# Mamba-2 scan in a fused diffusion block: masks joined to the decay matmuls, loads released by their last readers, skip term added by VectorE

## The reference, cut to what matters

```python
y = xs * lp["ssd_d"]                                   # the skip term
for d in range(2):                                     # forward, and backward on flipped tokens
    lower = jnp.tril(...)
    decay_in = jnp.exp(jnp.where(lower, a_cum[..., :, None] - a_cum[..., None, :], -jnp.inf))
    cb = jnp.einsum("bclgn,bcsgn->bgcls", cc, bc)
    y_diag = jnp.einsum("bgcls,bgecls,bcsgep->bclgep", cb, decay_in, xc)
    y_off = jnp.einsum("bclgn,cbgepn,bgecl->bclgep", cc, h_in, jnp.exp(a_cum))
    y = y + y_diag + y_off
```

## Time and profile before

| | |
|---|---|
| Median of 3 runs | 2537.04 us (2533.92 to 2537.75) |
| Profiled execution | 2539.05 us, span 2537.3 us |
| TensorE busy | 2397.6 us, 94% |
| VectorE busy | 1629.5 us, 64% |
| ScalarE busy | 940.6 us, 37% |
| GpSimd busy | 268.9 us, 11% |
| First instruction of the scan proper | 805.7 us |
| Last VectorE operation of the scan | 904.25 us |

### The profile page before, as it was taken

How to read it: one execution, slowest core, us unless ns; L and a number is a source line. 1 busy time by engine, 2 the same in 40 slices (tenths; PEclk the granted TensorE clock), 3 DMA queues, 4 the chain that set the end, 5 groups by cost and what they waited for, 6 DMA issues and landing times. The chain is left out here.

```text
span 2537.3 us, 30702 instructions
## 1 busy us (share of the span) xinstructions
PE 2397.6 (94%) x12041; PEld 1937.5 (76%) x12041; DVE 1629.5 (64%) x1679; ACT 940.6 (37%) x1099; POOL 268.9 (11%) x260
## 2 busy tenths in 40 slices
PE   6999899899999999999999999999599999999994
PEld 2468777678888978788787788868588888888882
DVE  7453389733344755324975536668888888888876
ACT  5133310233323533001112000031277777777764
POOL 0000000000143300000000001100012112121210
PEclk8999999999999999999999999999699999999997
DMA  5431155312344323111111115533699999999965
GB/s 203 164 124 42 47 190 179 111 46 84 116 150 138 100 65 104 44 52 50 42 50 38 42 50 168 180 140 117 258 360 368 368 357 366 360 371 390 385 265 204
DMA packets 93583, 437.12 MB, mean 172 GB/s; under 512 B 17080, under 2 KB 28616, under 8 KB 78762
## 3 DMA queue, kind: packets, MB, share of 16 engines
q1 hardware_dynamic: 64714, 349.02, 37.5%
q0 software_dynamic: 28768, 86.69, 9.9%
HBM read 401.12 MB, written 55.51 MB: 180 GB/s over the span
## 5 line engine op out<-in xcount | busy, mean ns | idle before, releaser
L390 PE MATMUL ps<-uT_upper_rest,ring_rest 128*128 128x512 f32 x1280 | 504.7, 394 | 0.0
L390 PE MATMUL ps<-uT_upper_rest,mix_upper 128*128 128x512 f32 x768 | 307.4, 400 | 9.9 <-DVE mix_val L2401 5.3
L390 PE MATMUL ps<-uT_rest,mix_upper 128*128 128x512 f32 x768 | 306.4, 399 | 0.0
L390 PEld LDWEIGHTS ps<-uT_upper_rest,ring_rest 128*128 128x128 f32 x1280 | 240.6, 188 | 61.1
L390 PEld LDWEIGHTS ps<-uT_upper_rest,mix_upper 128*128 128x128 f32 x768 | 145.5, 189 | 47.5 <-DVE mix_val L2401 5.7
L390 PEld LDWEIGHTS ps<-uT_rest,mix_upper 128*128 128x128 f32 x768 | 145.3, 189 | 33.0 <-issue 0.5
L1833 ACT ACTIVATE mix_gates<-ps 128x1024 f32<-128x1024 f32 x24 | 24.7, 1027 | 384.3 <-PE ps L390 367.3
L1884 DVE TENSOR_TENSOR mix_prod<-mix_gates,ps 128x1024 f32<-128x1024 f32 x24 | 29.3, 1221 | 211.1 <-PE ps L390 211.1
L2932 PE MATMUL ps<-ex_u_raw_rest,uT_rest 128*128 128x256 f32 x560 | 157.0, 280 | 0.0
L2930 PE MATMUL ps<-ring_rest,uT_rest 128*128 128x256 f32 (+1 forms) x416 | 135.1, 325 | 3.1 <-DVE uT_rest L3295 2.4
L2930 PE MATMUL ps<-ex_upper,uT_rest 128*128 128x256 f32 (+1 forms) x424 | 135.4, 319 | 0.0
(11 more groups left out here) (477 smaller groups left out, 5549.1 us busy)
## 6 DMA issues: line engine op xcount, KB each, us to landing
sb_spare<-in_ex_g SPq DMA_DIRECT2D x35, 2048.0 KB, 10.0
ex_u_raw<-in_ex_u SPq DMA_DIRECT2D x35, 2048.0 KB, 10.6
sb_merged<-in_ex_d SPq DMA_DIRECT2D x35, 2048.0 KB, 9.4
ring<-in_conv SPq DMA_DIRECT2D x32, 512.0 KB, 3.4
ring<-in_w_gate SPq DMA_DIRECT2D x32, 512.0 KB, 3.4
mix_piece<-in_w_late POOLq DMA_DIRECT2D x32, 512.0 KB, 5.2
ring<-in_w_ssd SPq DMA_DIRECT2D x20, 512.0 KB, 3.3
ring<-in_w_mod SPq DMA_DIRECT2D x16, 512.0 KB, 4.3
```

What stands on the lines that cost most here:

```text
L390: last = self.nc.tensor.matmul(out, weight, x[:, k, lo:hi], start=(k == 0 and n == 0), stop=(k == kt - 1 and n == 2))
```

## The change

Four things are changed.

1. *Masks.* Partitions 64 to 127 of `rows` now hold a constant, minus BIG on the diagonal of each 64-column block, and the weights `allowed(d, f)` hold ones for the row part and a 0/1 pattern for the mask part. One matmul gives mask and decay together, for one direction, four heads and half of the tokens (4 runs of 64 columns); a segment is one direction and four heads, two matmuls. The number of segments, banks and exponentials stays; their order becomes forward and backward alternately by four heads. The rows are loaded in three pieces. The second mask sum still waits for the last exponentials, the first for four segments instead of three. One segment (u = 3) moves ahead of `diagonal(n - 1, 1)`.
2. *Loads.* SP waits for each tile's last reader: `b_chan` and `c_chan` for `off_mm`, `b_tok` for `state_mm`, `xs` for `diag_mm` and `skip_ready`.
3. *Skip.* `skipped` goes; VectorE adds `skip` to `off` in SBUF, an eleventh operation per chunk, between backward off and the sum into y.
4. *Preparation.* `eye`, `ones` and `never` go; VectorE fills `rows` in two operations and `allowed` in seven.

The diff, cut to its core:

```diff
-        eye, ones = at_byte("eye", late + 36864, [P, P], F32R), at_byte("ones", late + 37376, [P, P], F32R)
-        never = at_byte("never", late + 37888, [P, 2, PAIR], F32R)
+
+        allowed_at = at_byte("allowed", late + 36864, [P, 2, 2, P], F32R)
+
+        def allowed(d, f):
+            return allowed_at[:, d, f, :]
...
-                    else:
-                        sp.wait_ge(y_done, n - 1)
-                    load_state(sp, n % 2, chunk(n), in_state[n % 2])
+                        load_state(sp, 1, chunk(1), in_state[1])
+                        load_out(sp, 1, in_out[1])
+                        continue
+                    sp.wait_ge(off_mm, 2 * (n - 1))
                     load_out(sp, n, in_out[n % 2])
+                    sp.wait_ge(state_mm, FIRST + n - 1)
+                    load_tok(sp, n % 2, chunk(n), in_state[n % 2])
+                    sp.wait_ge(diag_mm, 2 * (n - 1))
+                    sp.wait_ge(skip_ready, n - 1)
+                    load_xs(sp, n % 2, chunk(n), in_state[n % 2])
...
-                    pe.wait_ge(in_rows[u // 3], 16 * (n + 1))
-                    for d in range(2):
-                        out = ps[:, at_bank, d * PAIR:(d + 1) * PAIR]
-                        nc.tensor.matmul(out, eye[:, :], never[:, d, :], start=True, stop=False)
-                        mm = nc.tensor.matmul(out, ones[:, :], rows[:, d, u * PAIR:(u + 1) * PAIR], start=False, stop=True)
+                    quad, d = u // 2, u % 2
+                    pe.wait_ge(in_rows[quad], 16 * (n + 1))
+                    out = ps[:, at_bank, :].rearrange("p (h f t) -> p h f t", h=4, f=2)
+                    given = rows[:, d, quad * QUAD:(quad + 1) * QUAD].rearrange("p (h f t) -> p h f t", h=4, f=2)
+                    for f in range(2):
+                        mm = nc.tensor.matmul(out[:, :, f, :], allowed(d, f), given[:, :, f, :], start=True, stop=True)
                     mm.then_inc(seg_mm, 1)
...
-                def skipped(n, q):
-                    pe.wait_ge(skip_ready, n + 1)
-                    nc.tensor.matmul(ps[:, 3 + q, 0:half], k.const("ident"), skip[:, q * half:(q + 1) * half],
-                                     start=True, stop=False)
-
                 def diagonal(n, q):
                     pe.wait_ge(mixed, 2 * n + q + 1)
                     pe.wait_ge(in_state[n % 2] if n else state_first, 32 * max((n + 1) // 2, 1))
                     for e in range(6):
                         h = 6 * q + e
                         mm = nc.tensor.matmul(ps[:, 3 + q, e * HD:(e + 1) * HD], grow_f[:, n % 2, h, :],
-                                              xs[:, n % 2, h * HD:(h + 1) * HD], start=False, stop=(e == 5))
+                                              xs[:, n % 2, h * HD:(h + 1) * HD], start=True, stop=True)
...
-                pe.wait_ge(rounded, 4)
+                pe.wait_ge(rounded, 8)
                 segments(0, 0)
                 segments(0, 1)
                 pe.wait_ge(turned_ready, reads_until(items - 1) + 2)
                 segments(0, 2)
                 forward_out(0)
+                segments(0, 3)
...
-                    segments(n, 3)
                     segments(n, 4)
                     pe.wait_ge(off_read, 2 * n + 1)
                     states_out(n, 1)
                     segments(n, 5)
                     if n:
                         pe.wait_ge(y_done, n)
-                    skipped(n, 0)
                     diagonal(n, 0)
...
-                    skipped(n, 1)
+                    if n + 1 < CHUNKS:
+                        segments(n + 1, 3)
                     diagonal(n, 1)
...
-                    if m == convs + 2:
-                        act.wait_ge(raw_turned, 1)
-                        nc.scalar.copy(eye[:, :], k.const("ident")).then_inc(rounded, 1)
-                        nc.scalar.copy(ones[:, :], k.ones[:, :]).then_inc(rounded, 1)
...
                 def grow(n, u):
+                    quad, d = u // 2, u % 2
                     act.wait_ge(seg_mm, 6 * n + u + 1)
-                    if n == 0 and u == 4:
+                    if n == 0 and u == 5:
                         act.wait_ge(last_out, 32)
-                    if n >= 2:
-                        act.wait_ge(diag_mm, 2 * (n - 2) + u // 3 + 1)
-                    if n >= 1:
-                        act.wait_ge(summed, 2 * (n - 1) + u // 3 + 1)
-                    for d in range(2):
-                        for e in range(2):
-                            h = 2 * u + e
-                            dst = grow_b[:, h, :] if d else grow_f[:, n % 2, h, :]
-                            at_col = d * PAIR + e * P
-                            ins = nc.scalar.activation(dst, ps[:, SEG[(6 * n + u) % 3], at_col:at_col + P], ACT.Exp,
-                                                       bias=at("bias", chunk(n), d, h, h + 1))
+                    if n >= 2 and d == 0:
+                        act.wait_ge(diag_mm, 2 * (n - 2) + min(quad, 1) + 1)
+                    if n >= 1 and d == 1:
+                        act.wait_ge(summed, 2 * (n - 1) + min(quad, 1) + 1)
+                    for e in range(4):
+                        h = 4 * quad + e
+                        dst = grow_b[:, h, :] if d else grow_f[:, n % 2, h, :]
+                        ins = nc.scalar.activation(dst, ps[:, SEG[(6 * n + u) % 3], e * P:(e + 1) * P], ACT.Exp,
+                                                   bias=at("bias", chunk(n), d, h, h + 1))
                     ins.then_inc(grown, 1)
...
-                    nc.vector.tensor_scalar(rows[:, :, :].rearrange("p d (h t) -> p (d h) t", t=P),
-                                            k.ones[:, :].unsqueeze(1).broadcast_to([P, 2 * HEADS, P]), 0.0, None,
-                                            ALU.mult).then_inc(blank, 1)
-                    for d, kept in enumerate(("upto", "from")):
-                        nc.vector.tensor_scalar(never[:, d, :].rearrange("p (e t) -> p e t", e=2),
-                                                k.const(kept).unsqueeze(1).broadcast_to([P, 2, P]), 1.0, BIG, ALU.subtract,
+                    nc.vector.tensor_scalar(rows[0:P // 2, :, :].rearrange("p d (h t) -> p (d h) t", t=P),
+                                            k.ones[0:P // 2, :].unsqueeze(1).broadcast_to([P // 2, 2 * HEADS, P]), 0.0,
+                                            None, ALU.mult).then_inc(blank, 1)
+                    nc.vector.tensor_scalar(rows[UNDER, :, :].rearrange("p d (h t) -> p (d h) t", t=P // 2),
+                                            k.const("ident")[UNDER, UNDER].unsqueeze(1).broadcast_to(
+                                                [P // 2, 4 * HEADS, P // 2]), -BIG, None, ALU.mult).then_inc(rounded, 1)
+                    of_rows = allowed_at[0:P // 2, :, :, :].rearrange("p d f s -> p (d f) s")
+                    nc.vector.tensor_scalar(of_rows, k.ones[0:P // 2, :].unsqueeze(1).broadcast_to([P // 2, 4, P]), 1.0,
+                                            None, ALU.mult).then_inc(rounded, 1)
+                    for d, inside in enumerate(("from", "upto")):
+                        nc.vector.tensor_scalar(allowed(d, 1)[UNDER, :], k.const(inside)[UNDER, :], -1.0, 1.0,
+                                                ALU.mult, ALU.add).then_inc(rounded, 1)
+                        nc.vector.tensor_scalar(allowed(d, 0)[UNDER, 0:P // 2], k.const(inside)[UNDER, UNDER], -1.0, 1.0,
+                                                ALU.mult, ALU.add).then_inc(rounded, 1)
+                        nc.vector.tensor_scalar(allowed(d, 0)[UNDER, UNDER], k.ones[UNDER, 0:P // 2], 1.0 - d, None,
                                                 ALU.mult).then_inc(rounded, 1)
...
-                    v.wait_ge(grown, 6 * n + 3 * q + 3)
+                    v.wait_ge(grown, 6 * n + 4 + 2 * q)
...
+                    v.wait_ge(skip_ready, n + 1)
+                    tt(off[:, :], off[:, :], skip[:, :], ALU.add).then_inc(skip_added, 1)
+                    v.wait_ge(skip_added, n + 1)
                     tt(state_in(c), state_in(c), off[:, :], ALU.add).then_inc(y_begun, 1)
...
-                        pool.wait_ge(seg_mm, 6 * (n - 1) + 3 * q + 3)
-                    part = slice(q * half * 2, (q + 1) * half * 2)
+                        pool.wait_ge(seg_mm, 6 * (n - 1) + 2 * q + 2)
+                    part = slice(q * QUAD, (q + 1) * QUAD)
                     pool.dma_start(rows[0:2, :, part], by_chunk[:, chunk(n), :, part]).then_inc(in_rows[q], 16)
...
                         load_rows(n + 1, 0)
+                        load_rows(n + 1, 1)
                     pool.wait_ge(in_state[n % 2] if n else state_first, 32 * max((n + 1) // 2, 1))
                     if n:
-                        pool.wait_ge(diag_mm, 2 * n)
+                        pool.wait_ge(skip_added, n)
...
-                        load_rows(n + 1, 1)
+                        load_rows(n + 1, 2)
```

(18 more changed lines are left out.)

## The result

The changed kernel takes 2549.69 us (median of 5 runs, 2547.86 to 2552.93) against 2537.04 us (5 runs, 2533.92 to 2537.82): ratio 1.0053, 95% interval [1.0042, 1.0064]. It is 12.65 us slower; 2530 was predicted, with a range up to 2538. The profiled execution took 2552.93 us (span 2551.0), 13.88 more than that of before.

The account below looks back on a forecast made before the run. TensorE bounds the scan now, VectorE after the change; seven periods -10.5, first chunk +0.7, last chunk +1.0, preparation +2.0 sum to -6.8 us, from 2537.04 to 2530, range 2523.5 to 2538 (8 in 10).

Parts of the forecast that it names:

- The walk: VectorE's chain of operations per scan chunk, with the new add: period 10.25 us without a collision.
- the hole at L1601: VectorE's wait for the chunk state, 12.7 us in all; the added operation would almost exactly fill it.
- segment matmuls with gaps in their PSUM output: New scan segments might run slower than 0.12 us each; at 0.36 TensorE sets the pace, 2541 us; chance 0.05.
- T+7.52: Predicted place of VectorE's first mask sum, in us after the chunk's backward off product starts (T).
- A wait that the period then meets: First mask sum in each scan period waits 0.6 us for GpSimd's skip product; period taken as 10.8 us.
- rival 3: Both GpSimd products go ahead of the first mask sum: period 12.25 to 12.95 us, total 2540 to 2545; chance 0.10.
- a clock of 0.5 inside the scan: Listed sign that the forecast is wrong: TensorE's clock at 0.5 within the scan.
- First chunk: First mask sum waits 1.0 us for a fourth segment group, partly hidden by VectorE's idle time: +0.7 us.
- Preparation: Fills near 745 us delay GpSimd's load issues and so an early state that TensorE wants: +2.0 us.
- Last chunk: Nothing covers the new add before the last diagonal, where TensorE sits idle: +1.0 us.
- rival 2: No measurable change: long preparation (2.8 us), lower clock in the last chunk (+1.3), period 11.2; 2535 us; chance 0.23.
- rival 1: No collision between GpSimd's product and the mask sum, short preparation (+0.1): period 10.25, 2524.5 us; chance 0.17.

Follow-up runs that it names:

- experiment 1: Changed kernel plus one wait: GpSimd starts the skip product only after VectorE's first mask sum of the same chunk; 2529.21 us, ratio 0.9970.
- experiment 5: Changed kernel plus one wait: GpSimd starts the `xend` product, not the skip product, only after the first mask sum; 2531.48 us, ratio 0.9975.
- experiment 3: Changed kernel with 144 useless matmuls added: each chunk's sixth segment computed ten times, in TensorE's idle time; 2540.57 us, ratio 1.0009.
- experiment 6: Kernel of experiment 1 with three useless PSUM copies on VectorE ahead of each `take_diagonal` from the second chunk on; 2549.36 us, ratio 1.0043.
- experiment 8: Changed kernel, no wait added, second row load half between GpSimd's products, or whole behind both; 2559.89 and 2560.66 us.
- experiment 2: Changed kernel with the skip part undone: TensorE adds the skip term again, changed masks and loads kept; 2533.57 us, ratio 0.9990.

## Why the prediction was wrong

**The walk was right.** It gave a period of 10.25 us without the collision; experiment 1 measured 10.36; there the new add waits a little for `xend` (1.12 instead of 0.96). The eleventh operation did fill the hole at L1601: in chunks at full clock the update waits 0.22 us. ScalarE stayed just in time, the `c_chan` wait went, segment matmuls with gaps in their PSUM output are not slower (20 records of 256 columns in 2.68 us, 0.13 each; 0.12 before). The skip product was expected at T+6.6 to T+6.9 and came at T+6.9 (835.22 - 828.32), and the sum's place, T+7.52, was exact to 0.1 us.

**The step that failed: "A wait that the period then meets".** It let VectorE in after one GpSimd product, 0.6 us, on the evidence of the 716 us rows, and gave both products ahead of the sum 0.10. In the scan both go ahead in all six chunks: 2.0 to 2.2 us. Its price was right in rival 3 (2.0 us for a product at T+6.8, period 12.25; measured 12.40), and experiment 5, which builds the assumed order, measured 10.98 for the assumed 10.8 and 2531.48 us for the predicted 2530. The evidence was one pair in another stage, with another VectorE operation; what it left out is that in the scan the second product is already queued, with nothing to wait for. At 716 us it was not: its load of `b_tok` was issued at 712.30 and landed 5.4 us later, at 717.7, when L1490 (717.26) had already asked.

**What no case had priced: the clock inside the scan.** Rival 3 kept TensorE at full clock and ended at 2540 to 2545. But a bound that moves to VectorE leaves holes in TensorE's work, and behind a first hole of 1.43 us and holes of 2.25 to 2.42 us the clock fell in five of seven periods. Experiment 3 shows the price (8.0 us in seven periods, 9 in the median) and experiment 6 that the hole is enough, without a collision. The prediction named a clock of 0.5 inside the scan as a sign of error, and priced it only for the last chunk.

The seven periods, in terms: the walk 7 x (10.36 - 12.30) = -13.6 (predicted -14.35); six collisions, 18.3 us of mask sums less 6 x 0.95 = +12.6 (predicted 7 x 0.55 = +3.85); the rest +8.3 (predicted 0), of which 7.8 is the clock: experiment 3, at full clock, has only 85.41 - 7 x 10.36 - 6 x (3.01 - 0.95) = 0.5 left beyond walk and collisions. Together +7.3 for the predicted -10.5.

**The ends.** First chunk: +0.7, as predicted. Preparation: predicted +2.0, measured 1.2 (the last early state's sum starts at 804.09 instead of 802.91); the second fill held GpSimd's issues (2.93 us for three), the seven small operations did not. Last chunk: predicted +1.0, measured +2.3, because TensorE idles 3.33 us and then does the diagonal in 2.79 us at the lower clock; rival 2 had 1.3 for this. After the scan 2.2 us more are lost, where 0 was predicted. The next stage starts at a clock of 0.50 in both kernels, but stays there for 14 of its matmuls after the change (920.12 to 926.26, 0.43 apart) and for 9 before (908.60 to 912.60); at full clock they are 0.23 apart, so this is 5 x 0.20 = 1.0 us. After the change the clock is at 0.50 once more from 1035.5 to 1038.8 us, where it stays at 1.00 before; why was not tested.

The Trainium skill (TensorE: Matmul & The Clock Gate, "Part 1: The HAM clock gate") says that activity releases the throttle and idle time brings it back. Experiments 3 and 6 agree; but no rule on the hole's length can be read from these traces: in the change the clock stayed up behind two holes of 2.51 and 2.52 us, and in experiment 6 it fell behind all five of 2.54.

One sum of the prediction is off: its 0.64 for a faster kernel is more than the 0.17 of rival 1 and nine tenths of the forecast's 0.50 give together, 0.62.

## What to carry to other kernels

Before moving an operation with two SBUF operands to VectorE, or anything that shifts VectorE against GpSimd, lay both engines' timelines on each other and price the meeting at the full length of *all* GpSimd products that are queued without a wait. Then look for the cheapest wait that puts GpSimd's work into VectorE's PSUM-reading stretch: in experiment 1 the three VectorE operations with a PSUM operand that run beside the products (842.19, 843.06 and 843.93) take 0.95 us each, and that one line was worth 20 us. And where the bound moves away from TensorE, price the hole by its clock too: the holes behind the collision cost 8 us on top of its own 12.6.

## What the runs showed of the hardware that was not expected

*Who gets the shared read path.* In all 12 meetings of a VectorE operation with both queued products in the change and in the skip part alone, and in the 12 of experiment 8, VectorE came last. It did so even where a DMA issue of 0.58 us stood between the products, and even where its record began 0.33 us before GpSimd's (831.98, 832.31). In experiment 2 it won with a record that began 0.23 us before (829.63, 829.86), from an idle start, while in experiment 8 it came straight behind another operation. The Trainium skill (SBUF — State Buffer, "Who interferes with whom") says that the shared ports are an exclusive lock, which whoever issues first has for the whole instruction. The lengths agree, but it does not say who is next when two wait.

The rows of 716 us show VectorE between two products. There the second product, and the load that it waited for (us from issue to landing: 5.4):

```profile
718.52 2.45 POOL L1610 TENSOR_TENSOR ssd_xend<-ssd_xs,sb_dt_dt_to_end 128x768 f32<-128x768 f32 x1
```

```profile
ssd_b_tok<-xbc_tok POOLq DMA_DIRECT2D x1, 256.0 KB, 5.4
```

One reading fits all these cases: first goes the instruction whose last wait was met first. At 716 us VectorE asked at 717.26 and the second product's data landed at 717.7. In experiment 2 GpSimd stood idle until TensorE released its product, just before 829.86, when the mask sum of 829.63 had begun. In the change and in experiment 8 nothing that GpSimd's products waited for was still open. This reading is argued from the times; no experiment tested it. One product's length is safe as a price only where just one product is free to go (1.59 us for the sum in experiment 5).

*More matmuls, less time.* 144 added matmuls made the changed kernel 9 us faster.
